# Two model stages on one Trainium2 core: where the spatial gate's bias is added, how the first weights arrive, and the order of the last products

## The reference, cut to what matters

```
p       = rmsnorm(h, pre) @ w_in                 # u, v, z of the spatial gate among the parts
v       = layernorm(v, ln_g, ln_b)               # per block of 128 rows, 8 groups of 64 features
s[g]    = w_s[g] (lower triangle) @ v[g] + b_s[g]    # one bias per group and row
y_sgu   = u * s * silu-like gate z
k_rope  = k * cos + swapped k * sin              # rope tables, also for q
h       = h + rmsnorm(mixed @ w_out, post_g)     # the end of each block
```

## Time and profile before

| | us |
|---|---|
| median of three runs | 945.93 |
| lowest, highest | 945.59, 949.43 |
| the profiled execution, its own time | 948.21 |
| its span, first to last instruction | 946.5 |
| TensorE matmuls busy in the span | 925.4 (98%) |
| TensorE weight loads | 862.3 (91%) |
| VectorE | 691.4 (73%) |
| ScalarE | 520.6 (55%) |
| GpSimd | 225.8 (24%) |
| mean granted TensorE clock | 0.994 |

### The profile page before, as it was taken

How to read it: one execution, slowest core, us unless ns; L and a number is a source line. 1 busy time by engine, 2 the same in 40 slices (tenths; PEclk the granted TensorE clock), 3 DMA queues, 4 the chain that set the end, 5 groups by cost and what they waited for, 6 DMA issues and landing times.

```text
span 946.5 us, 19686 instructions
## 1 busy us (share of the span) xinstructions
PE 925.4 (98%) x7966; PEld 862.3 (91%) x7966; DVE 691.4 (73%) x1063; ACT 520.6 (55%) x941; POOL 225.8 (24%) x194
## 2 busy tenths in 40 slices
PE   8999999989999999999999999999899999999997
PEld 7999888979999988789999899998699998999995
DVE  6988875477999895567878675576659787655684
ACT  8653465456556664564665565544646565554443
POOL 3445221430221221004223130042033132300140
PEclk9999999989999999999999999999999999999999
DMA  8543200236555555456534535555284444545551
GB/s 318 179 157 112 75 20 2 78 101 199 181 178 184 182 180 189 159 206 247 175 125 144 172 124 192 181 187 192 83 307 156 157 157 133 168 159 188 182 176 45
DMA packets 41562, 150.21 MB, mean 159 GB/s; under 512 B 4608, under 2 KB 4864, under 8 KB 41216
## 3 DMA queue, kind: packets, MB, share of 16 engines
q1 hardware_dynamic: 39456, 141.54, 44.8%
q10 hardware_dynamic: 2016, 7.41, 2.2%
HBM read 147.88 MB, written 1.05 MB: 157 GB/s over the span
## 4 chain that ended last, share of the span: by engine, by line
PE 92%; DVE 3%; ACT 2%; issue 2%; POOL 1%; DMA 0%; DVEq 0%; SPq 0%; ACTq 0%; POOLq 0%
PE ps L728 89%; PE ps L1063 2%; ACT whi L1280 1%; DVE wlo L1696 1%; PE ps L1169 1%; ACT xh L1280 0%; DMA raw<-in_ws 0%; DVE S L1696 0%; ACT tmp L1280 0%; ACT L1280 0%; POOL ocf L2276 0%; DVE ht L1704 0%; DVE pcraw L1696 0%; POOL fS L2276 0%; DVE rr L1738 0%
## 5 line engine op out<-in xcount | busy, mean ns | idle before, releaser
L1280 ACT ACTIVATE whi<-raw 128x1024 fp32r<-128x1024 f32 (+1 forms) x264 | 278.1, 1055 | 297.2 <-PE ps L728 289.5
L728 PE MATMUL ps<-xh,whi 128*128 128x256 f32 (+2 forms) x1440 | 413.7, 287 | 4.0 <-DVE wlo L1696 1.4
L1696 DVE TENSOR_TENSOR wlo<-raw,whi 128x1024 fp32r<-128x1024 f32 (+1 forms) x256 | 324.0, 1269 | 119.9 <-ACT whi L1280 119.0
L728 PE MATMUL ps<-xl,whi 128*128 128x256 f32 (+2 forms) x1440 | 408.2, 283 | 1.6 <-DVE xl L1704 1.6
L728 PE MATMUL ps<-xh,wlo 128*128 128x256 f32 (+2 forms) x1440 | 407.4, 283 | 0.0
L728 PEld LDWEIGHTS ps<-xh,whi 128*128 128x128 f32 x1440 | 272.1, 189 | 10.6 <-issue 8.6
L728 PEld LDWEIGHTS ps<-xl,whi 128*128 128x128 f32 x1440 | 271.5, 189 | 2.8 <-DVE xl L1704 2.2
L728 PEld LDWEIGHTS ps<-xh,wlo 128*128 128x128 f32 x1440 | 272.5, 189 | 0.0
L2276 POOL TENSOR_TENSOR gts<-gts 128x256 f32<-128x256 f32 x32 | 30.2, 955 | 150.5 <-DVE gts L1704 149.9
L728 PE MATMUL ps<-yh,whi 128*128 128x256 f32 x232 | 65.3, 281 | 0.0
L728 PE MATMUL ps<-yl,whi 128*128 128x256 f32 x232 | 65.2, 281 | 0.0
(11 more groups left out here) (345 smaller groups left out, 1327.8 us busy)
## 6 DMA issues: line engine op xcount, KB each, us to landing
raw<-in_ws SPq DMA_DIRECT2D x262, 512.0 KB, 3.4
h<-in_rel ACTq DMA_DIRECT2D x2, 1024.0 KB, 13.5
qc<-in_gam ACTq DMA_DIRECT2D x3, 512.0 KB, 5.2
mt<-in_m ACTq DMA_DIRECT2D x2, 576.0 KB, 6.1
h<-in_hT SPq DMA_DIRECT2D x4, 272.0 KB, 5.5
gts<-in_lng ACTq DMA_DIRECT2D x2, 512.0 KB, 8.3
out<-ht SPq DMA_DIRECT2D x4, 256.0 KB, 2.0
gts<-in_g ACTq DMA_DIRECT2D x2, 448.0 KB, 10.3
```

The lines of the kernel that those rows point to most:

```text
L728: return e.matmul(o, l, r, start=start, stop=stop, skip_group_check=True)
L1280: return e.activation(o, a, f, bias=bias, scale=scale, accum_out=acc)
L1696: return e.tensor_tensor(o, a, b, op)
```

## The change

The diff has five parts.

1. The spatial gate's bias: `bs` is laid out as 128x512 on the host, `e8` goes, `sgu` loses its four bias products, and VectorE adds the bias out of the bank in `y_first` before its multiply. `k3` shrinks by 256 KB, `mt3` grows by 192 KB.
2. `g3` (rope tables) is issued first of a layer's constants.
3. Unit 0 is loaded, copied and subtracted in two halves of 512 columns; the first half's load is SyncE's first, and TensorE waits for halves. The pulse of the first entry has 9 products in place of 14.
4. In the last block of rows of the last layer, half 0 of the features takes its last three units ahead of half 1; ScalarE's square of half 1 no longer waits for VectorE, and VectorE multiplies half 0 first and half 1 after the sum.
5. The strings of the two layers, and those of the mixer by the one added step, are new. In layer 0 the attention turns move earlier or closer together, in layer 1 a few of them, and the rotary key comes one tile earlier.

```diff
-C3 = Layout([("cmask", 256), ("e8", 512)])
-M3 = Layout([("ws", 1024), ("bs", 128)])
+C3 = Layout([("cmask", 256)])
+M3 = Layout([("ws", 1024), ("bs", 512)])
...
-        return [("split", self.cut - 1)]
+        return [("split", 0, 0), ("split", 0, 1)] if self.cut == 1 else [("split", self.cut - 1)]
...
-                if i == 0:
+                if u == 0 and i == 4 or u and i == 0:
                     pe.wait_ge(("w.hi", u), ("w.lo", u))
...
+                    if st == 0 and k == 0:
+                        pe.wait_ge(("w.hi.half",), ("w.lo.half",))
...
-                for i in range(14):
+                for i in range(14 if st else 9):
...
+            def last_turns(j, b, k):
+
+                last = PROJ[j] - LEAD
+                if j < 3 or not b or k < last:
+                    return [(0, k), (1, k)]
+                return [[(0, last), (0, last + 1), (0, last + 2)], [(1, last), (1, last + 1)], [(1, last + 2)]][k - last]
...
-                pe.wait_ge(("va.t", l, b), ("ws.t", l), ("d.k3",))
-                for m in range(4):
-                    o = ps[:, m * 128:(m + 1) * 128]
-                    mm(o, c3v("e8")[0:8, m * 128:(m + 1) * 128], m3v("bs")[0:8, :], m == 0, False)
+                pe.wait_ge(("va.t", l, b), ("ws.t", l))
...
-                if i:
+                if i and not ends(j, b):
                     sc.wait_ge(("ng", j, b, 1))
...
+                e.dma_start(g3_at, g3[l, :, :]).then_inc(*sc.lands("d_g3", ("d.g3", l)))
                 if l == 0:
                     e.dma_start(k3[:, :], c3).then_inc(*sc.lands("d_k3", ("d.k3",)))
                 e.dma_start(mt3[:, :], m3[l, :, :]).then_inc(*sc.lands("d_m3", ("d.m3", l)))
                 e.dma_start(lnr, lng[l, :, :].partition_broadcast(128)).then_inc(*sc.lands("d_ln", ("d.ln", l)))
-                e.dma_start(g3_at, g3[l, :, :]).then_inc(*sc.lands("d_g3", ("d.g3", l)))
...
+                if nm[0] == "s":
+                    d.wait_ge(("d.m3", l))
+                    tt(yf[i], src, pairs(m3v("bs")[:, 128 * rows.start:128 * rows.stop]), ADD).then_inc(
+                        *d.says(("y.b", nm, t), frees=key))
+                    d.wait_ge(("y.b", nm, t))
+                    src, key = yf[i], None
                 stt(yf[i], src, 0.5, zs[:, rows, q0:q0 + 128], MUL, MUL).then_inc(*d.says(("y.f", nm, t), frees=key))
...
+            def times_gain(j, b, x):
                 d.wait_ge(("tile", ("ot", j, b, x)), ("d.gam", j))
-                if x == 0:
-                    d.wait_ge(("nq", j, b, 0))
+                if x == 0 or ends(j, b):
+                    d.wait_ge(("nq", j, b, x))
...
                     tt(nsum[:, b, 0:1], nsum[:, b, 0:1], nsum[:, b, 1:2], ADD).then_inc(*d.says(("nr.s", j, b)))
+                    if ends(j, b):
+                        times_gain(j, b, 1)
...
             def init():
+                load_half(0)
                 for i in range(4):
                     e.dma_start(h[:, 2 * i:2 * i + 2, :],
                                 hT[:, 2 * i * T:(2 * i + 2) * T].rearrange("p (k t) -> p k t", k=2)).then_inc(
                         *s.lands(f"d_h{i}", ("d.h", i)))
-                    load(i)
+                    if i:
+                        load(i)
+                    else:
+                        load_half(1)
```

The strings of TensorE (d a dense tile or a smaller product, e and o attention steps, t the rotary key, s the gate), as far as they differ:

```diff
 layer0
-            "dddddtdtdddddeoddddddddddddddddoeeeodeodoeoeeooddedeeeedoddoedeoeddddeeoddddddoodooeddedooosodsddd"
+            "dddddtdtdddddeoododddddddddeeeddeoddoddeooeeoddedeedodooeoeedeeeeddddddddddddoodooeoodedddodossddd"
 layer1
-            "ddddddtdtddddeoooeddddddddddeeddeododddeoeeooddedeeodooooddddeeedeoeedooooeededododddddddddddssddd"
+            "dddddtdtdddddeoooeddddddddddeeddeododddeoeeooddedeeeedodooeoodeeedoddooooeededoddddoddddddddddssddd"
```

More of the change, by code:

```diff
@@ L705, in program, with cols_of, part @@
         tile_banks = (PJ0, PJ1, PJ2, PJ2)
-        def cols_of(u):
-            return slice(0, 512 if u in half_units else 1024)
+        def cols_of(u, x=None):
+            return slice(0, 512 if u in half_units else 1024) if x is None else slice(512 * x, 512 * x + 512)
+        def part(what, u, x):
+            return (f"{what}.half",) if x == 0 else (what, u)
         def on_pool(u):
@@ L719, in half, with ends @@
             return slice(n * i, n * i + n)
+        def ends(j, b):
+            return j == 3 and b == 1
         def tensor(pe):
@@ L1132, in out_tokens @@
                 pe.wait_ge(("w.hi", u), ("w.lo", u), *evs)
[L1133 to L1142, removed]
+                o = ps_of(("ot", j, b, x))[:, :]
+                mm(o, a, whi[:, u % NSPL, half(x)], k == 0, False)
+                mm(o, c, whi[:, u % NSPL, half(x)], False, False)
+                t = mm(o, a, wlo[:, u % NSPL, half(x)], False, k == n - 1)
+                said = ([("tile", ("ot", j, b, x))] if k == n - 1 else []) + ([("w.used", u)] if b and x else [])
+                if said:
+                    t.then_inc(*pe.says(*said))
             def first_values(l, b, i):
@@ L1286, in init, with split @@
                 e.dma_start(cst[:, :], c0).then_inc(*sc.lands("d_c0", ("d.c0",)))
-            def split(u):
+            def split(u, x=None):
                 if u >= NSPL:
                     sc.wait_ge(("w.used", u - NSPL))
-                sc.wait_ge(("d.w", u))
-                c = cols_of(u)
-                act(whi[:, u % NSPL, c], raw[:, u % NRAW, c], ACT.Copy).then_inc(*sc.says(("w.hi", u)))
+                sc.wait_ge(part("d.w", u, x))
+                c = cols_of(u, x)
+                act(whi[:, u % NSPL, c], raw[:, u % NRAW, c], ACT.Copy).then_inc(*sc.says(part("w.hi", u, x)))
             def enter(st, k):
@@ L1719, in init2, with split @@
                 tt(wfl[:, :], m1v("wf"), wfh[:, :].bitcast(F), SUB).then_inc(*d.says(("fo.wl",)))
-            def split(u):
+            def split(u, x=None):
                 if on_pool(u):
                     return
-                d.wait_ge(("w.hi", u))
-                c = cols_of(u)
+                d.wait_ge(part("w.hi", u, x))
+                c = cols_of(u, x)
                 tt(wlo[:, u % NSPL, c], raw[:, u % NRAW, c], whi[:, u % NSPL, c].bitcast(F), SUB).then_inc(
-                    *d.says(("w.lo", u)))
+                    *d.says(part("w.lo", u, x)))
             def enter(st, k):
@@ L2475, in load, with load_half @@
                     e.dma_start(raw[:, u % NRAW, c], ws[u, :, c]).then_inc(*s.lands(f"s_w{u % NRAW}", ("d.w", u)))
+            def load_half(x):
+                c = cols_of(0, x)
+                e.dma_start(raw[:, 0, c], ws[0, :, c]).then_inc(
+                    *s.lands("s_w0" if x else "s_half", part("d.w", 0, x)))
             def init():
+                load_half(0)
                 for i in range(4):
@@ L2493, in store @@
                 s.wait_ge(("out", 3))
-            do = {"init": init, "split": lambda u: load(u + NRAW), "store": store}
+            do = {"init": init, "split": lambda u, x=1: load(u + NRAW) if x else None, "store": store}
             for step in engine_order("sp", do):
@@ L2578, in consts @@
     put(G3, g3, "rm", rm)
-    e8 = np.zeros((8, 512))
-    for g in range(8):
-        e8[g, g * 64:g * 64 + 64] = 1
-    put(C3, c3, "e8", e8)
     return c0, c1, c3, np.stack([g3, g3])
```

61 lines of the change are left out of this document (35 added, 26 removed).

## The result

The changed kernel ran in 942.22 us (median of eight, 941.05 to 944.58), the kernel before beside it in 946.67 us (944.86 to 949.43): ratio 0.9953, 95% interval 0.9940 to 0.9966, so 4.45 us less (3.2 to 5.7). The forecast was 5.1 us less.

What follows compares the result with a forecast made beforehand. TensorE was taken to bound the layers, latency the entry and end. Terms -4.3 + 0.4 - 0.65 - 0.5 = -5.1 us took the median 945.93 to 940.8 us, range 938 to 944.

Steps and rivals of the forecast that it cites:

- its chances: Whole kernel: faster by over 0.5% (below 941.2) 0.5, within 0.43, slower by over 0.5% 0.07.
- Bias products: Spatial gate on TensorE: four groups of bias products at 1.08 us each go, 4.3 us less.
- VectorE's additions: Gate: eight bias additions of about 0.36 us, 2.8 us in all, hidden under dense tiles, cost nothing.
- Seams: Layers' new strings: one more stretch of fp32 steps between dense ones in each layer, cost 0.4 us.
- The gate's v: Second gate product needs GpSimd's v: room 0.2 us in layer 1; zero stalls taken, bounds 0 to 3 us.
- Rival (b): Gate's v a little late, layer 1 room 0.2 us: 1 to 3 us back, 942 to 944; chance 0.17.
- the prediction's signs: TensorE idle before a gate product or the fifth gate tile, released by GpSimd's v, would show a late v.
- Entry: From first load to root: ScalarE starts earlier, then meets unit 2's load; gain 0.65 us, bounds -1 to 2.2.
- End: Behind the last matmul: earlier square of half 1 and last multiply, gain 0.5 us, bounds 0.2 to 0.8.
- (c): Gate's v late in full: TensorE stalls 3.2 us in layer 0, 5.7 in layer 1, 949.7 us; chance 0.06.
- (e): Entry gives the full 2.2 us, as later loads are also early: 939.3 or less; chance 0.07.
- (d): Entry gives nothing or costs 1 us, TensorE staying at 1.2 GHz beyond 9.3 us: 941.5 to 942.5; chance 0.1.

Runs made afterwards that it cites:

- e1: The kernel before with only the gate's bias moved from TensorE to VectorE (part 1); 942.61 us, ratio 0.9964 to before.
- e2: The kernel before with the new strings of both layers and `g3` first, bias products kept; 948.37 us, ratio 1.0019 to before.
- e8: The changed kernel with tile 4 ahead of unit 2, lam's small steps behind the root, unit 3's copy behind the last tile; 941.06 us, ratio 0.9936 to before.
- e3: The kernel before with only the entry changed (halves, nine pulses, the mixer's strings); 946.43 us, ratio 1.0005 to before.
- e6: The changed kernel with feature tile 4 ahead of unit 2 on ScalarE and VectorE; 941.28 us, ratio 0.9939 to before.
- e4: The kernel before with only the end changed (part 4); 945.82 us, ratio 0.9990 to before.
- e12: The fastest entry (reordered ScalarE, VectorE and GpSimd steps, 14 pulses) on the changed kernel, with layer 1's old strings; 940.94 us, ratio 0.9938 to before.

## Why the prediction was right, and where it was not

The forecast, 940.8 us from 945.93, was 5.1 us less and just beyond 0.5%; 4.45 us, 0.47%, was measured, just within, which its chances left nearly open. The time lies in its range. By its steps:

- **Bias products, -4.3:** right. -4.4 in e1, as the rows have it. The estimate of 3.6 us, from the 56 ns from start to start that the Trainium skill gives for a warm matmul of 128 columns (TensorE: Matmul & The Clock Gate, Part 1), was too low.
- **VectorE's additions, 0:** right; 0.41 or 0.42 us each where 0.36 was taken, all under dense tiles.
- **Seams, +0.4:** near in sum, +0.3 in e2, by luck: the seams and the moved turns came to +0.07 in layer 0 and -0.16 in layer 1, and the other 0.42 us are the wait at the output matrix, which the prediction put at nothing. Beside the bias edit the new strings gained 0.10 us in layer 0 (251.98 for e1's 252.08) and cost 0.25 in layer 1.
- **The gate's v, 0:** right, by luck: the wait in layer 1 is 0.06 us. Rival (b) had the place right, and there was less room than its 0.2 us. One stall is there in layer 0, and the prediction's signs had its place but not its cause: the fifth gate tile starts at 552.74, some 0.3 us late, for a bank that VectorE empties from 552.28 on. v was done at 550.94, so VectorE did not wait for it; it was busy to 552.02 with two weight remainders, 1.72 and 2.30 us beside GpSimd's work on v:

```profile
548.08 3.94 DVE L1713 TENSOR_TENSOR wlo<-raw,whi 128x1024 fp32r<-128x1024 f32 x2
```

In layer 1 VectorE does wait 1.23 us for v (the row at 820.00), and TensorE is not held.
- **The Trainium skill's rule** (SBUF — State Buffer, Who interferes with whom) is that a VectorE operation with two SBUF inputs and a GpSimd operation that reads SBUF block each other. In the entry the rows agree again, 2.31 us beside GpSimd's 2.38, and in e8 a VectorE operation of only 64 columns took 2.36 us beside it. The gate's multiply, which the prediction feared for, took 0.43 us, and GpSimd's four operations 8.05, as in the earlier trace rows; the two small stalls that did come, 0.3 us in layer 0 and 0.42 in layer 1, stand behind weight remainders that took 1.72 to 2.30 us beside GpSimd's work, where 1.2 is usual.
- **Entry, -0.65:** the step that failed. The prediction let unit 2 land at 3.10 + 6.8 = 9.9, as before; but SyncE issues it at 3.58 now, and it landed at 10.40 here and 10.70 in e3, and ScalarE, ahead by its early start, waited for it. With the later issue alone the prediction's own sum would have given 10.4. The rest of that step came nearly as worked out, the first copy at 3.83 (3.5), the copy of unit 1 at 8.55 (8.46). The root gained 0.14 us against a profile of before whose first load was the latest of four, so nothing that can be told.
- **End, -0.5:** -0.63; the square begins 0.43 us behind the last matmul's start, and the multiply 0.15 us sooner than worked out.
- **Not in the sum:** +0.37 us of the last store (below).

In the profile that is -4.26 for the two layers, -0.14, -0.63, +0.37 and +0.20 in the mixer: -4.46 besides the 1.40 of clock, and 4.45 was measured by the medians. That the two meet so closely is luck too, as the equal-clock value is -4.9 +- 0.6. (c), the slower case, did not happen in either layer; (e) could not, as later loads were not early. Of (d) the outcome came, an entry that gives nothing and a time of 942.2, but in the changed kernel not its cause; TensorE at 1.2 GHz in the entry came in e6.

## What to carry to other kernels

Work taken from a full engine is time gained nearly in full (4.4 us for 4.3); work taken from the front of a latency chain is worth nothing until each next wait is named and moved: here the load of unit 2, then three table loads, then a GpSimd step in the wrong order, next to nothing for the first edit and 0.6 to 0.9 us for all of them. A small loss that fits a forecast should still be looked up where it lies: the 0.26 us taken for seams were a wait at another place. Small steps that nobody needs soon (lam) should stand behind the root that everybody waits for. And where executions scatter by 2 us through the clock, the stages of one profile, with their clock beside them, tell apart what ten timed runs can't; but a stage that begins with a load needs more than one profile, as the same entry came out 0.3 to 0.4 us apart.

## What was not expected of the hardware

**The last store.** The page's DMA issues, of the changed kernel and of e4 (which lacks the bias edit), with the median time to landing last:

```profile
out<-ht SPq DMA_DIRECT2D x4, 256.0 KB, 2.4
```

```profile
out<-ht SPq DMA_DIRECT2D x4, 256.0 KB, 2.0
```

The four stores take 2.4 us in e1 and 2.0 in the kernel before. The span behind the last multiply is 3.57 or 3.58 us in all ten kernels with the bias edit and 3.19 to 3.21 in the four without. The edit touches no store. It changes the sizes of two constants and may so move tensors in memory; whether that is the cause was not tried.

**The clock outside the change.** Every profile has 3.4 or 6.8 us at 1.2 GHz in the mixer near 200 to 207, two also near 401 and three near 670, all where TensorE had pauses of 0.4 to 1.6 us shortly before. Three (the changed kernel, e4, e12) have 3.4 or 6.8 us near 152 to 155 as well, and there TensorE had made small fp32 products without a pause; the other profiles have the same work there at full clock. e1 and e2, which touch only the layers, had lower mean clocks (0.9934, 0.9928) than before, e3 and e4 (0.9955, 0.9949, 0.9958). With one profile each the extra half-clock time can't be placed; the cause stays open.
